# Last item's rows added to the output tiles on TensorE, inside the loop's last round

## What is computed

```python
def moe_ffn(xn, ...):                       # n = 1024 tokens, 32 experts, top 4 of them
    top_val, top_idx = lax.top_k(logits, 4)
    gates = softmax(top_val)
    # token slots sorted by expert, in blocks of 128; for each block:
    gu = xb @ w_gu[e] + b_gu[e]
    h = (clip(u, -7, 7) + 1) * (min(g, 7) * sigmoid(1.702 * g))
    yb = h @ w_down[e] + b_down[e]
    # y[token] += yb * gate
h = h + moe_ffn(rmsnorm(h, g_ffn))
out = rmsnorm(h, final_norm_g)
```

## Time and profile before

| | |
|---|---|
| median of 3 runs | 2191.32 us (2190.98 to 2191.32) |
| profiled execution | 2194.93 us, span 2193.2 us |
| TensorE matmul busy | 2120.9 us, 97% |
| VectorE, ScalarE, GpSimd busy | 1578.9, 1264.3, 436.7 us |
| mean granted clock of TensorE | 0.981 |
| memory traffic in the steady loop | 342 GB/s |

### The profile page before, as it was taken

The page is one execution under the profiler, slowest core; times in us unless marked ns, Lnnn a source line. Parts: engine busy times, 40 slices in busy tenths (PEclk is TensorE's granted clock), DMA queues, the critical chain, the costliest instruction groups (busy, mean ns, idle before and its releaser), DMA issues.

```text
span 2193.2 us, 33019 instructions
## 1 busy us (share of the span) xinstructions
PE 2120.9 (97%) x9638; PEld 1671.3 (76%) x9639; DVE 1578.9 (72%) x1490; ACT 1264.3 (58%) x1217; POOL 436.7 (20%) x366
## 2 busy tenths in 40 slices
PE   7999999999997799999999999999999999999995
PEld 4464878887685688888888888888888888888883
DVE  5745682406537798687879977987889779987794
ACT  3135451415323577667667766776677667776673
POOL 0693000000002122122121212221222122231120
PEclk9999999999997899999999999999999999999998
DMA  5101351111234799899799979999999789998995
GB/s 179 39 1 61 134 192 39 39 39 39 70 143 144 271 373 375 313 331 336 275 328 380 381 285 328 382 376 336 330 326 382 284 321 370 379 383 302 326 357 188
DMA packets 233560, 555.76 MB, mean 253 GB/s; under 512 B 19972, under 2 KB 20072, under 8 KB 232296
## 3 DMA queue, kind: packets, MB, share of 16 engines
q1 hardware_dynamic: 218304, 512.28, 63.1%
q0 software_dynamic: 13248, 42.50, 7.7%
q10 hardware_dynamic: 1960, 0.35, 0.1%
HBM read 518.12 MB, written 33.69 MB: 252 GB/s over the span
## 4 chain that ended last, share of the span: by engine, by line
PE 92%; DVE 4%; issue 2%; ACT 1%; DMA 1%; ACTq 1%; DVEq 0%; POOLq 0%; POOL 0%
PE PS L1010 25%; PE PS L649 19%; PE PS L1014 14%; PE PS L1049 12%; PE PS L1056 6%; PE PS L815 4%; PE PS L855 4%; PE PS L1002 2%; PE PS L1081 2%; PE PS L951 2%; PE PS L667 1%; DVE WA L1561 0%; DVE WL L1999 0%; PE PS L793 0%; DMA y_acc<-WA 0%
## 5 line engine op out<-in xcount | busy, mean ns | idle before, releaser
L1999 DVE TENSOR_TENSOR WL<-WA,WH 128x2048 fp32r<-128x2048 f32 x288 | 654.8, 2292 | 48.9 <-ACT WH L1415 22.7
L1999 DVE TENSOR_TENSOR WL<-H,WH 128x2048 fp32r<-128x2048 f32 x144 | 328.5, 2288 | 64.3 <-ACT WH L1527 34.4
L1010 PE MATMUL PS<-WH,XEH 128*128 128x512 f32 x1344 | 363.1, 392 | 1.7 <-DVE WL L1999 1.7
L1014 PE MATMUL PS<-WL,XEH 128*128 128x512 f32 x1344 | 353.2, 391 | 0.0
L1438 ACT CAST WH<-WA 128x2048 fp32r<-128x2048 f32 x140 | 267.3, 1910 | 145.5 <-PE PS L1056 129.1
L1010 PE MATMUL PS<-WH,XEL 128*128 128x512 f32 x1152 | 310.7, 392 | 0.0
L1010 PEld LDWEIGHTS PS<-WH,XEH 128*128 128x128 f32 x1344 | 254.4, 189 | 54.4 <-DVE WL L1999 2.6
L1014 PEld LDWEIGHTS PS<-WL,XEH 128*128 128x128 f32 x1344 | 253.6, 189 | 53.0
L1010 PEld LDWEIGHTS PS<-WH,XEL 128*128 128x128 f32 x1152 | 218.0, 189 | 46.4
L1049 PE MATMUL PS<-WH,HTH 128*128 128x512 f32 x672 | 187.1, 400 | 3.2 <-ACT WA L1495 3.2
L1420 ACT CAST WH<-WA 128x2048 fp32r<-128x2048 f32 x70 | 133.7, 1910 | 82.9 <-PE PS L1014 66.6
(11 more groups left out here) (347 smaller groups left out, 2785.9 us busy)
## 6 DMA issues: line engine op xcount, KB each, us to landing
WA<-in_exp_w_gu SPq DMA_DIRECT2D x216, 1024.0 KB, 9.4
H<-in_exp_w_gu SPq DMA_DIRECT2D x72, 1024.0 KB
WA<-in_exp_w_down SPq DMA_DIRECT2D x72, 1024.0 KB, 9.2
H<-in_exp_w_down SPq DMA_DIRECT2D x72, 1024.0 KB, 9.2
WB<-in_xa_wkv SPq DMA_DIRECT2D x4, 2048.0 KB, 8.1
WB<-in_w_in SPq DMA_DIRECT2D x3, 2048.0 KB, 9.3
y_acc<-H SPq DMA_DIRECT2D x9, 512.0 KB, 2.7
H<-in_x SPq DMA_DIRECT2D x4, 1024.0 KB, 5.9
```

The source lines that it names most:

```text
L1010: nc.tensor.matmul(PS[:, 2 * h + t, :], x[:, KT4 * half + k, t * P:(t + 1) * P], WH[:, j % 4, k * HALF:(k + 1) * HALF], start=False, stop= ...
L1014: ins = nc.tensor.matmul(PS[:, 2 * h + t, :], XEH[:, KT4 * half + k, t * P:(t + 1) * P], WL[:, j % 4, k * HALF:(k + 1) * HALF], start=Fals ...
L1999: v.tensor_tensor(WL[:, s, :], src, WH[:, s, :].bitcast(F32), sub).then_inc(done, 1)
```

## The change

The last item's rows no longer go through `y_acc`. In the last round ScalarE scales the down products to `YH` and VectorE makes the low part `YL`. VectorE compares the item's token numbers (`TKL`) with the column numbers to one-hot matrices `OHL`, one per row tile, and TensorE multiplies these with `YH` and `YL` into the row tile's PSUM pair (`last_rows`). GpSimd's `store` is left out in that round. So SyncE loads `y_acc` when item 34's rows have landed (`ys_free` i), in four parts of two row tiles, but the norm vector behind the same wait. The whole tail of TensorE, ScalarE and VectorE moves into the branch of the last round, `loop_left` is gone, and VectorE adds rows for tile 7 as well. `GT3` and `BD3` move to other buffers, and the tail's transposes between the halves of the down products.

With it come: `gate_up` stands at the start of round i, for item i, with `slot_list` in a branch of it, and `first_item` is gone; each weight piece is waited for in two steps (`gu_high` ahead of the products with `WH`, `gu_low` ahead of those with `WL`); each `down` half waits for its own half of `HTL`; and in the first round VectorE does `gate_up_low(5)` ahead of `slot_tables`.

```diff
-        acc_part = ((0, 1), (1, 2), (2, 5), (5, L))
-        ON_DVE = (1, 3, 5)
+        acc_part = ((0, 2), (2, 4), (4, 6), (6, L))
+        ON_DVE = (1, 3, 5, 7)
+        OUT_BANK = (2, 0, 6, 4)
...
+                        sp.wait_ge(ys_free, i)
                         sp.dma_start(FG, A["final_norm_g"].partition_broadcast(P)).then_inc(tail_in, 16)
-                        sp.wait_ge(ys_free, i + 1)
                         for n, (l0, l1) in enumerate(acc_part):
+                            if n == 0:
+                                sp.wait_ge(gu_low, 8 * i)
+                            elif n > 1:
+                                sp.wait_ge(dn_low, 4 * i + n + 3)
...
+                def gate_up(tiles):
+                    pe.wait_ge(sel_done, i + 1)
...
+                        elif u == 2:
+                            with pe.If_cmp(n_p, 0, "IS_GT"):
+                                pe.wait_ge(gate_done, 2 * i + 1)
+                            with pe.Else():
+                                slot_list()
+                                pe.wait_ge(gate_done, 1)
...
+                            pe.wait_ge(gu_high, 8 * i + j + 1)
...
+                            pe.wait_ge(gu_low, 8 * i + j + 1)
...
+                def last_rows(l, tiles):
+                    parts = [(OHL[:, 0, l, :], YH), (OHL[:, 0, l, :], YL)]
+                    if tiles == 2:
+                        parts += [(OHL[0:HP, 1, l, :], YH1[0:HP]), (OHL[0:HP, 1, l, :], YL1[0:HP])]
+                    for n, (hot, y) in enumerate(parts):
+                        if l == 0 and n == 1:
+                            pe.wait_ge(y_low, 1)
+                        for c in range(2):
+                            ins = nc.tensor.matmul(PS[:, OUT_BANK[l % 4] + c, :], hot, y[:, c * HALF:(c + 1) * HALF],
+                                                   start=False, stop=n == len(parts) - 1)
+                    ins.then_inc(sum_filled, 1)
+
+                def rows_out(tiles):
+                    pe.wait_ge(bd3_done, 1)
+                    pe.wait_ge(dve_tail, 2)
+                    for l in range(2):
+                        gated_bias(l)
+                    loaded_rows(0)
+                    pe.wait_ge(dve_tail, 3)
+                    pe.wait_ge(y_done, i + 1)
+                    for l in range(L):
+                        if l > 1:
+                            gated_bias(l)
+                        if l not in ON_DVE and l:
+                            loaded_rows(l)
+                        last_rows(l, tiles)
+
+                by_tiles(pe, n_i, gate_up)
                 counts.fetch(i)
                 by_tiles(pe, n_n, next_tokens(0))
                 by_tiles(pe, n_p, down(0))
                 by_tiles(pe, n_n, next_tokens(1))
-                by_tiles(pe, n_i, hidden_transposes(0))
+                by_tiles(pe, n_i, hidden_transposes(0), gated_transposes)
                 by_tiles(pe, n_p, down(2))
-                by_tiles(pe, n_i, hidden_transposes(1))
-                by_tiles(pe, n_n, next_item)
...
+                by_tiles(pe, n_i, hidden_transposes(1), lambda: by_tiles(pe, n_p, rows_out))
...
+                def last_y():
+                    act.wait_ge(gu_used, 8 * i + 4)
+                    act.wait_ge(tail_in, 64)
+                    nc.scalar.copy(BD3, BDN[0:3 * E, :]).then_inc(bd_high, 1)
+                    act.wait_ge(gated_filled, 1)
+                    for h in range(2):
+                        nc.scalar.copy(GT3[:, h * HALF:(h + 1) * HALF], PS[0:3 * E, h, :]).then_inc(gt_high, 1)
+                    act.wait_ge(dn_used, 4 * i + 8)
+                    act.wait_ge(ys_free, i)
+                    act.wait_ge(gs_in, 32 * i)
+                    nc.scalar.activation(YH, PS[:, 4:6, :].rearrange("p a b -> p (a b)"), ACT.Copy, scale=GSC[:, 0:1]) \
+                        .then_inc(y_done, 1)
...
+                with dve.If_cmp(n_i, 0, "IS_GT"):
+                    by_tiles(dve, n_p, add_y)
+                with dve.Else():
+                    with dve.If_cmp(n_p, 0, "IS_GT"):
+                        last_rows()
...
-                by_tiles(pool, n_p, store)
+                with pool.If_cmp(n_i, 0, "IS_GT"):
+                    by_tiles(pool, n_p, store)
```

More of the change, by code:

```diff
@@ L983, in slot_list @@
                 ins.then_inc(list_done, 1)
[L985 to L1028, removed]
             pe.wait_ge(itm_done, 1)
             counts = Counts(pe, "pe")
-            by_tiles(pe, counts.here, first_item)
+            with pe.If_cmp(counts.here, P, "IS_GT"):
+                banks_read((1, 3))
+                pe.wait_ge(wide0_in, 16)
+                for half in range(2):
+                    ins = tile_tokens(half, 1)
+                ins.then_inc(wide0_step, 1)
+                pe.wait_ge(wide0_step, 3)
@@ L1083, in hidden_transposes, with gated_transposes, gated_bias @@
                     return part
-                def next_item(tiles):
-                    gate_up(i + 1, tiles)
+                def gated_transposes():
+                    pe.wait_ge(gf3_done, 1)
+                    for l in range(L):
+                        ins = nc.tensor.transpose(PS[0:3 * E, l // 4, (l % 4) * P:(l % 4 + 1) * P], GF3[:, l, :], ident[:])
+                    ins.then_inc(gated_filled, 1)
+                def gated_bias(l):
+                    if l >= 4:
+                        pe.wait_ge(out_ready, l - 3)
+                    for c in range(2):
+                        nc.tensor.matmul(PS[:, OUT_BANK[l % 4] + c, :], GT3[:, l * P:(l + 1) * P], BD3[:, c * HALF:(c + 1) * HALF],
+                                         start=True, stop=False)
@@ L1522, in _ @@
                 by_tiles(act, n_i, hidden(1))
-                by_tiles(act, n_p, keep_y)
+                def last_y():
[10 more added lines that the diff above has]
+                        .then_inc(y_done, 1)
+                    with act.If_cmp(n_p, P, "IS_GT"):
+                        nc.scalar.copy(Y1[0:HP], PS[HP:P, 6:8, :].rearrange("p a b -> p (a b)")).then_inc(y_moved, 1)
+                        act.wait_ge(y_added, i)
+                        nc.scalar.activation(YH1[0:HP], Y1[0:HP], ACT.Copy, scale=GSC[0:HP, 1:2]).then_inc(y_moved, 1)
+                    nc.scalar.preload_act_table(ACT.Sqrt)
+                    for l in range(L):
+                        pair = OUT_BANK[l % 4]
+                        if l in ON_DVE:
+                            act.wait_ge(dve_tail, 4 + ON_DVE.index(l))
+                            y = ACC[:, l, :]
+                        else:
+                            act.wait_ge(sum_filled, l + 1)
+                            y = PS[:, pair:pair + 2, :].rearrange("p a b -> p (a b)")
+                        a(SQ[:, l % 2, :], y, ACT.Square, accum_out=sm[:, l:l + 1])
+                        a(sm[:, l + 8:l + 9], sm[:, l:l + 1], ACT.Sqrt, bias=sm[:, 127:128], scale=1.0 / D, s=ssq_done[4])
+                with act.If_cmp(n_i, 0, "IS_GT"):
+                    by_tiles(act, n_p, keep_y)
+                with act.Else():
+                    last_y()
                 with act.If_cmp(n_n, 0, "IS_GT"):
@@ L1527, in _ @@
                     nc.scalar.copy(WH[:, 0, :], raw_gu(4)).then_inc(gu_high, 1)
[L1528 to L1544, removed]
         @block.vector
@@ L2362, in _ @@
             with items(pool, counts) as i:
+                n_i = counts.here
                 n_p = counts.before
```

145 lines of the change are left out of this document (86 added, 59 removed).

## The result

| | before | after |
|---|---|---|
| median | 2191.32 us | 2387.09 us |
| lowest to highest | 2190.98 to 2195.49 | 2385.64 to 2387.98 |
| ratio, 95% interval | | 1.0884 [1.0871, 1.0896] |
| span of the profiled run | 2193.2 | 2386.3 |
| mean granted clock of TensorE | 0.981 | 0.954 |

The prediction said 2198.5 us with a range up to 2206. Three instants of the timelines cut both spans alike: the first product of the second item (A, the last line of the earlier trace rows), the issue of item 34's store (B, the first of the earlier trace rows) and the end of the last scaling (C, the last of the earlier trace rows).

A forecast was written before the change was run, and what follows sets the result against it. TensorE was taken to bound the loop, full from 780 to 2140 us. Span 2193.2 + 6.2 (tail and exit) + 1 (start) = 2200.4; that difference added to the median gave 2198.5 us, own range 2195.5 to 2202, wider 2191.5 to 2206.

The forecast's parts named there:

- The loop taken as untouched: Loop, 780 to 2140 us: TensorE busy 1359.11 of 1360 us, so the change could act only outside that stretch.
- Rival 4: Loop: grown code no longer stays loaded, so each of 35 rounds stalls; over 70 us, above 2260; 4 in 100.
- The removed chain and the loads: Before the tail: last scatter and loads behind it go; SyncE's loads follow item 34's scatter, norm vector there about 2155.1.
- The gather of the gates: Last round: gate values are the late input, 7 us in full queues (bounds 2.35 and 7.3); YL ready at 2164.2.
- The row tiles: Tail: 4.6 us per pair of row tiles, last scaling ending at 2184.2 against today's 2189.1.
- rival 3: Tail: TensorE stays at half clock; one pair adds 4.6 us, 2203, all three give 2212; 6 in 100.
- The exit: After the tail: VectorE leaves the loop after its last scaling, 15.2 us with the closing barrier; +6.2 us, serial.
- Rival 1: Program end: VectorE's exit is not on the path, the output's landing ends the span; 2187.3 us; 8 in 100.
- The start: Second item's start: 4.12 us stall stays, +1.5 for round-end bookkeeping, -0.6 for an earlier wait removed; about +1 us.
- rival 2: Second item's start: the stall goes away as the loop's gate_up is warm; about -3 us, 2194.5; 22 in 100.
- Separate waits for WH and WL: 0: Gate-and-up products: TensorE may begin on WH alone, but waits for neither in the steady loop; 0 us.
- slower: Whole kernel: the outcome slower than before, as against faster (0.05) or within measurement's 0.2% (0.25); given 0.70.

The follow-up runs named there:

- e1: The changed kernel, with ScalarE loading the gate function's table again after the tail's last root: 2199.02 us, ratio 1.0032 to before.
- e3: e1 with VectorE also skipping the empty rounds (each=True): 2190.08 us, ratio 0.9991 to before.
- c1: The kernel before, with VectorE alone made to skip the empty rounds: 2193.01 us, ratio 1.0003.
- e8: e3 with GROUP = 8 and VectorE's last_rows moved behind the loop: 2185.31 us, ratio 0.9967 to before.
- e6: e3 with TensorE's rows_out ahead of the second hidden transposes in the code, execution order unchanged: 2191.02 us, ratio 0.999 to before.
- e9: e8 with TensorE's rows_out moved behind its loop too: 2182.12 us, ratio 0.9951 to before.
- e7: e6 with GROUP = 8 in place of 4, so three unused groups are stepped over, not six: 2189.89 us, ratio 0.9991 to before.

## Why the prediction was wrong, by its own steps

**The loop taken as untouched: the step that failed.** "Nothing that another engine does there is worth anything, and no part of the change takes products away there" was read from TensorE's full stretch, and the change was then looked for at the start, in the last round and in the tail alone. A full bound says that less work elsewhere gains nothing; it does not say that more work elsewhere costs nothing. Nowhere was it asked what the build adds on ScalarE when functions of another table move into the loop, and the sum had no term for it: 181.9 us, 276 table loads and TensorE's waits for the gate behind them. One of the prediction's own signs of being wrong had been "any wait of TensorE between 780 and 2140". What could have warned stood in the trace of before, on ScalarE's timeline in the tail, behind the loop:

```profile
2164.66 1.28 ACT L1534 ACT_TABLE_LOAD   x1
```

That load is the square root's, and the diff moves its cause into a branch of the loop. Rival 4 named the right kind of thing, a cost of every round above 2260 us with 4 in 100, by the wrong mechanism: instruction loading. In after no branch of TensorE takes over 213 ns between the second item and 2320 us; its reason against, that today's loop stays loaded, held.

**The removed chain and the loads: right.** With 184.2 us taken off after's instants (the later issue of the store), the norm vector is issued at 2151.5, behind the landing of item 34's scatter, and is there at 2156.3 where 2155.1 was said. ScalarE waited for it (its copies write `XEH` and `XEL` by the trace's names):

```profile
2327.76 3.34 POOL L2454 DMA_INDIRECT y_acc<-WA  x1 [26.83 <-ACT WA L1514]
2335.66 0.36 SPq L618 DMA_DIRECT2D H<-in_final_norm_g  x1
2339.27 1.02 POOL L2431 DMA_INDIRECT WA<-gate_rows,WA  x1 [0.85 <-POOL WA L2427]
2340.51 1.28 ACT L1545 ACT_TABLE_LOAD   x1 [13.57 <-DMA H<-in_final_norm_g]
2344.71 1.11 ACT L1552 ACTIVATE WAR<-PS,WA 128x1024 fp32r<-128x1024 f32 x1 [0.89 <-DMA WA<-gate_rows,WA]
2345.57 1.49 PE L1105 MATMUL PS<-XEH,XEL 96*128 96x512 f32 x4 [3.77 <-DVE XEL L2229]
2346.86 3.25 PE L1111 MATMUL PS<-WA,ident 128*128 128x512 f32 x4
2347.66 1.28 DVE L2247 SCALAR_TENSOR_TENSOR WAR<-PS,WA,WAR 128x1024 fp32r<-128x1024 f32 x1
...
2368.61 1.28 DVE L1594 SCALAR_TENSOR_TENSOR WA<-WA,sm,H 128x1024 f32<-128x1024 f32 x1
```

**The gather of the gates: late for YH, but not the last input.** 7 us were taken, 5.4 measured (2339.27 to 2344.71), and it was the late input of YH, as said. It was not what the tail waited for. VectorE's preparation, which the sum had beside the gather, came last, held up by a table load and the later norm vector. YL came at 2163.5 on before's scale, 0.6 later than the forecast's 2162.9 and 1.8 us behind the end of YH, and TensorE's first bias products waited for the same preparation.

**The row tiles: right.** A pair took 4.5 us (4.6 said). The last scaling ends at 2185.7 on before's scale, 1.5 behind the 2184.2; in e1 B to C is 38.6 against the 40.6 of the sum. The 3.5 us between e1 and after are about those of the table load at L1545 (1.3), of the norm vector, issued 7.9 and not 7.0 us behind the store, and of the slower first products described under rival 3 (1.4).

**The exit: right, 1.2 us short** (16.4 for 15.2), on the path as e3 shows and free in before as c1 shows. Rival 1 falls with it. "Serial: no later wait can cover it" holds while the tail stands in the loop; in e8 an earlier wait covers it.

**The start: the stall stayed, right.** In e1 the gap is 4.13 us for 4.12, and rival 2 falls. The 0.60 us wait ahead of the first item's fourth quarter is gone in e1. The 1.5 us for the round's bookkeeping did not come: from the last transposes to the first product it is 5.25 us in e1 and 5.24 in before. That the jump across `rows_out` is the one that is paid is shown by e6 and e9.

**"Separate waits for WH and WL: 0"** could not be told from zero (A to B 1397.9 in e1 and 1397.5 in before).

**Rival 3, half clock in the tail: it came for one row tile.** TensorE had stood idle for 3.77 us in after. Its granted clock was 0.50 from 2347 to 2349, and the first tile's four passes with the loaded rows took 3.25 us. In e1 they took 1.88, behind 1.16 us of idle time and at a clock of 1.00. From 2350 on the clock is full and a pair takes 4.5 us, so it cost 1.4 us and not the 4.6 of a whole pair.

So the parts that were looked at were summed to 2198.5 us where e1 has 2199.0, and the forecast failed by 188 us on a part that was not looked at. That the two agree to 0.5 us is partly luck: the forecast's span of 2200.4 is 2.6 over e1's 2197.8. Start and tail came 2.2 and 2.0 us shorter than said, exit and loop 1.2 and 0.4 longer, and the start alone differs by 1.2 us between before and c1, where it is unchanged (A at 746.09 and 744.94). Nor does the "slower" that had 0.70 bear the prediction out: its reason is worth the 0.3% of e1, and the 8.8% have another.

## What to carry to other kernels

Before a function moves into or out of a loop or branch, list ScalarE's functions of each block by their table, and see that all ways that meet leave the same table loaded; if not, reload it at the end of the rare branch, which costs 1.28 us once. A bound that is full only tells what less work is worth elsewhere, so for each engine ask how much more a round can take before the bound waits (here 2.6 to 4.8 us in an ordinary round, nothing in six of them). Work that ends a program is best placed behind the loop, where the way out of the loop lies beside a wait that is there anyway.

## What was not expected of the hardware

- A function-table load takes 1.283 us each time, with no further pause behind it (0.02 us at 1250.03); eight in each round, through TensorE's wait for one gate, made 188 of the 196 us (e1).
- A gap of 4 us on TensorE costs more than itself: in after the next four products took 1.91 us and not 1.07, at a granted clock of 0.50. The same shows in the tail: the four passes with the first loaded rows took 1.88 us in e1 and e6, behind 1.1 to 1.2 us of idle time, and 3.0 to 3.5 us in after, e3, e7, e8 and e9, behind 2.4 to 3.8. Of the 184.2 us that the store came later, 127 are idle time of TensorE (130.9 against 3.9) and 57 slower products.
- The same first jump across code that has not run took 3.2 to 3.7 us at the end of the round (e8, e3, after) and 5.7 to 5.9 us a little earlier in it (e6, e7). The Trainium skill, "Runtime: NRT & Kernel Launch", section "Instruction fetch mechanics", has it that a taken branch to code outside what is loaded waits for a fetch; e9, where nothing in the loop jumps across the sums and no such stall is seen, agrees, and what sets the length is open.
- A step of VectorE over one empty group or round takes 0.75 us, all of it the sequencer's own (three rounds and six groups between 2181.4 and 2188.4 in e3).
